# A decoder step on one core: level products merged in the recurrence, prompt attention reordered two heads ahead

## What is computed

```python
# recurrence, per head, one token at a time
sa = einsum('bhij,bhj->bhi', S, -kk_t)
S = S * w_t[:, :, None, :] + sa[..., None] * (kk_t * a_t)[:, :, None, :] + v_t[..., None] * k_t[:, :, None, :]
y = einsum('bhij,bhj->bhi', S, r_t)
# attention of the prompt, per head and branch
s = einsum(q, k) * HEAD_DIM ** -0.5 - slopes * dist          # masked where dist < 0
o = gates[0] * softmax(s_cmp) @ v_cmp + gates[1] * softmax(s_slc) @ v_slc + gates[2] * softmax(s_win) @ v_win
```

## Time and profile before

| | us |
|---|---|
| median of 3 runs | 2620.49 (2618.21 to 2624.07) |
| the profiled execution | 2620.29 |
| its span, first to last instruction | 2618.5 |
| recurrence, from its first matmul to the last chunk's `sa_product` | 214.1 |
| prompt attention | 75.0 |
| from the end of the output projection on | 1058 |

### The profile page before, as it was taken

The page is one execution under the profiler, slowest core; times in us unless marked ns, Lnnn a source line. Parts: engine busy times, 40 slices in busy tenths (PEclk is TensorE's granted clock), DMA queues, the critical chain, the costliest instruction groups (busy, mean ns, idle before and its releaser), DMA issues. The chain is left out here.

```text
span 2618.5 us, 48741 instructions
## 1 busy us (share of the span) xinstructions
PE 2294.2 (88%) x20955; PEld 1646.5 (63%) x20955; DVE 741.7 (28%) x2064; ACT 343.0 (13%) x776; POOL 74.0 (3%) x123
## 2 busy tenths in 40 slices
PE   6899999799999777786776997999999999999996
PEld 4577676677777666755654764566566666556663
DVE  1111211340141245455654124112111112221115
ACT  1001100211210000014322012001010000001001
POOL 0000000000000000001011010000000000000000
PEclk9999999899999967777788998999999999999998
DMA  9987886533444420036468217999999999999990
GB/s 323 346 320 270 332 333 235 163 106 106 129 129 129 120 81 5 5 75 165 159 259 338 78 48 314 424 426 427 426 416 424 426 419 425 426 416 423 424 396 37
DMA packets 205116, 687.62 MB, mean 263 GB/s; under 512 B 38986, under 2 KB 85019, under 8 KB 165371
## 3 DMA queue, kind: packets, MB, share of 16 engines
q1 hardware_dynamic: 195746, 642.59, 62.9%
q0 software_dynamic: 7056, 38.29, 4.3%
q10 hardware_dynamic: 2180, 4.76, 0.5%
HBM read 687.16 MB, written 19.86 MB: 270 GB/s over the span
## 5 line engine op out<-in xcount | busy, mean ns | idle before, releaser
L2761 PE MATMUL bank<-sb_gate_w,sb_x_picked 128*64 128x256 f32 x2048 | 331.2, 389 | 53.6 <-DMA sb_up_w<-in_w_up_dram 53.6
L647 PE MATMUL bank<-sb_hT,sb_sample_kv 128*128 128x296 f32 (+1 forms) x1408 | 355.5, 412 | 12.3 <-PEq L494 12.3
L2761 PE MATMUL bank<-sb_up_w,sb_x_picked 128*64 128x256 f32 x2048 | 330.1, 387 | 0.0
L647 PEld LDWEIGHTS bank<-sb_hT,sb_sample_kv 128*128 128x128 f32 x1408 | 267.9, 191 | 94.7 <-issue 17.5
L2761 PEld LDWEIGHTS bank<-sb_gate_w,sb_x_picked 128*64 128x64 f32 x2048 | 175.4, 140 | 125.8 <-issue 81.7
L2786 PE MATMUL bank<-sb_down_w,sb_hiddenT 128*64 128x512 f32 x1024 | 226.8, 594 | 9.0 <-ACT sb_x_picked L2843 9.0
L469 PE MATMUL bank<-sb_cmp_xT,sb_cmp_w 128*128 128x254 f32 x1024 | 223.3, 379 | 6.6 <-ACT sb_cmp_xT L241 5.8
L469 PEld LDWEIGHTS bank<-sb_cmp_xT,sb_cmp_w 128*128 128x128 f32 x1024 | 193.2, 190 | 38.1 <-ACT sb_cmp_xT L241 7.3
L2761 PEld LDWEIGHTS bank<-sb_up_w,sb_x_picked 128*64 128x64 f32 x2048 | 179.2, 140 | 49.0 <-issue 1.0
L2913 DVE TENSOR_TENSOR sb_hidden<-sb_hidden,bank 128x256 f32<-128x256 f32 x32 | 13.5, 421 | 688.8 <-ACT sb_hidden L2851 688.8
L2786 PEld LDWEIGHTS bank<-sb_down_w,sb_hiddenT 128*64 128x64 f32 x1024 | 84.1, 137 | 129.0 <-issue 115.4
(11 more groups left out here) (569 smaller groups left out, 2340.2 us busy)
## 6 DMA issues: line engine op xcount, KB each, us to landing
sb_gate_w<-in_w_gate_dram SPq DMA_DIRECT2D x64, 2048.0 KB, 16.4
sb_up_w<-in_w_up_dram SPq DMA_DIRECT2D x64, 2048.0 KB, 18.7
sb_down_w<-in_w_down_dram SPq DMA_DIRECT2D x64, 2048.0 KB, 18.2
sb_w_ada<-in_w_ada_dram SPq DMA_DIRECT2D x48, 2048.0 KB, 10.9
sb_sample_kv<-in_w_in_dram SPq DMA_DIRECT2D x22, 2048.0 KB, 8.0
sb_sample_kv<-in_cache_cmp_kv_dram SPq DMA_DIRECT2D x128, 256.0 KB, 7.4
sb_sample_kv<-in_w_out_dram SPq DMA_DIRECT2D x16, 1024.0 KB, 12.2
sb_sample_kv<-in_state_win_kv_dram SPq DMA_DIRECT2D x8, 1024.0 KB, 16.3
```

What stands on the lines that cost most here:

```text
L647: ins = pe.matmul(bank[j % 4][:, 0:wide], ch[:, t, j % 2 * P:(j % 2 + 1) * P], hT[:, t, 0:wide], start=(t == 0), stop=(t == KT - 1))
L2761: ins = pe.matmul(bank[b][64 * half:64 * half + 64, col:col + 256], x[:, t, b * 64:b * 64 + 64], w[i][:, t % CK, half * 256:half * 256 + 256],
```

## The change

Three edits.

1. Recurrence. `pw` gets a third slot, which holds the running sum. Powers and sum are now neighbours, so the products of line 1049 and line 1053 at levels 1 and 2, which have the same stationary operand, become one matmul of 64 columns. All products of a level go to bank 3. Over a chunk, 176 level products become 144. DVE's add writes the sum into the other `pw` tile, and at level 4 into `u.pt`.
2. Prompt attention. The query scale moves into the copies at the end of the input projection (lines 785 and 879), so `scaled` goes. Scores of the selected and window branch become one matmul per tile, the values five matmuls of up to 256 columns instead of eight, DVE's two distance terms one instruction, and the factors of both tiles one pair of instructions. The copy of the compressed part's transpose and `written` move from DVE to ACT. PE issues `scores(0)`, `scores(1)` and then `turned(h)`, `scores(h+2)`, `values(h)`.
3. The samples' queries are multiplied by 1.0 instead of the scale (line 1851).

```diff
@@ phase_in, ACT and DVE @@
-                        act.copy(k.pT[:, j - N_R, 0:NT], bank[j % 4][:, 0:NT]).then_inc(s_copy[0], 1)
+                        act.activation(k.pT[:, j - N_R, 0:NT], bank[j % 4][:, 0:NT], ACT.Copy,
+                                       scale=SCALE if j - N_R < HEADS else 1.0).then_inc(s_copy[0], 1)
...
-                        dve.tensor_copy(k.pT[:, j - N_R, 0:NT], bank[j % 4][:, 0:NT]).then_inc(s_copy[1], 1)
+                        dve.tensor_scalar(k.pT[:, j - N_R, 0:NT], bank[j % 4][:, 0:NT], SCALE if j - N_R < HEADS else 1.0,
+                                          None, ALU.mult).then_inc(s_copy[1], 1)
@@ phase_scan @@
-        pw = [sb(f"pow{i}", [P, 2, Q, CL]) for i in range(2)]
+        pw = [sb(f"pow{i}", [P, 3, Q, CL]) for i in range(2)]
...
-                    if i < 3:
-                        for h in range(HT):
-                            _, _, q, rb = head(h)
-                            ins = pe.matmul(bank[3][rb, P + q * CL:P + (q + 1) * CL], cur[rb, 0, q, :], cur[rb, 1, q, :], start=True, stop=True)
-                    if i > 0:
-                        for h in range(HT):
-                            _, _, q, rb = head(h)
-                            ins = pe.matmul(bank[5][rb, q * CL:(q + 1) * CL], cur[rb, 0, q, :], u.pt[rb, q, :], start=True, stop=True)
+                    lo, hi = (1 if i < 3 else 2), (3 if i > 0 else 2)
+                    for h in range(HT):
+                        _, _, q, rb = head(h)
+                        ins = pe.matmul(levels[rb, lo:hi, q, :], cur[rb, 0, q, :], cur[rb, lo:hi, q, :], start=True, stop=True)
                     ins.then_inc(s_lp, 1)
...
-                        ins = dve.tensor_tensor(full(u.pt), full(u.pt), bank[5][:, 0:P], ALU.add)
+                        sum_ = u.pt[:, :, :] if i == 4 else nxt[:, 2, :, :]
+                        ins = dve.tensor_tensor(fl3(sum_), fl3(cur[:, 2, :, :]), bank[3][:, 2 * P:3 * P], ALU.add)
@@ phase_attend_prompt @@
+                    for t in range(2):
+                        pe.matmul(k.bank[t][:, 0:2 * NK[t]].rearrange("p (a n) -> p a n", a=2), k.pT[:, h, t * P:(t + 1) * P],
+                                  k.pT[:, SLC_T + g:WIN_T + g + 1:WIN_T - SLC_T, 0:NK[t]], start=True, stop=True).then_inc(s_s, 1)
...
                 scores(0)
+                scores(1)
                 for h in range(HEADS):
-                    if h + 1 < HEADS:
-                        scores(h + 1)
                     turned(h)
+                    if h + 2 < HEADS:
+                        scores(h + 2)
                     values(h)
...
+                exps(0, 0)
+                exps(0, 1)
+                normed(0)
+                exps(1, 0)
+                exps(1, 1)
                 for h in range(HEADS):
-                    normed(h)
+                    cmp_copied(h)
                     if h + 1 < HEADS:
-                        exps(h + 1)
+                        normed(h + 1)
+                    if h + 2 < HEADS:
+                        exps(h + 2, 0)
+                    written(h)
+                    if h + 2 < HEADS:
+                        exps(h + 2, 1)
...
                 biased(0)
+                biased(1)
+                factors(0)
                 for h in range(HEADS):
-                    factors(h)
+                    copied(h)
                     if h + 1 < HEADS:
-                        biased(h + 1)
+                        factors(h + 1)
                     if h + 2 < HEADS:
-                        scaled(h + 2)
-                    if h:
-                        written(h - 1)
-                    copied(h)
-                written(HEADS - 1)
+                        biased(h + 2)
```

More of the change, by code:

```diff
@@ new lines, in biased @@
+                        both = lambda w: w.rearrange("p (a n) -> p a n", a=2)
+                        dve.scalar_tensor_tensor(out=v[:, 0:NCP], in0=dcmp[:, t, :], scalar=sl,
+                                                 in1=k.bank[0][:, TP + 16 * t:TP + 16 * t + NCP], op0=ALU.mult, op1=ALU.add)
+                        step(dve.scalar_tensor_tensor(out=both(v[:, 16:16 + 2 * nk]), in0=dist, scalar=sl,
+                                                      in1=both(k.bank[t][:, 0:2 * nk]), op0=ALU.mult, op1=ALU.add))
```

100 lines of the change are left out of this document (45 added, 55 removed).

## The result

| | before | after |
|---|---|---|
| median of five runs, us | 2620.49 (2615.68 to 2625.64) | 2607.70 (2599.71 to 2610.61) |
| the profiled execution | 2620.29 | 2599.71 |
| its span | 2618.5 | 2598.0 |

The ratio is 0.9946, with a 95% interval of 0.9923 to 0.9969, so the changed kernel is faster, by 12.8 us by the medians (8 to 20 us by the interval). The forecast of 2599.3 us lies 8.4 us under the median. That it lies within half a microsecond of the profiled execution is luck: that execution is the fastest of the five, the others took 2607 to 2611 us.

The account below looks back on a forecast made before the run. The prediction took PE's instruction arrival to bound the recurrence, and PE's waits, then SP's DMA stream, the prompt attention: 2620.3 - 11.5 - 9.5 = 2599.3 us, with a range of 2592 to 2612 us.

Parts of the forecast that it names:

- The bound of the recurrence: Recurrence: PE waits for its instructions, arriving in pieces of 256 about every 3.5 us; a chunk can't take under 22.2 us.
- Rival 1: Recurrence: stops stay, only PE's own time counts, about 1 us gained; 2610 us, chance 0.17.
- The size of that term: Recurrence: half a piece of 256 instructions fewer per chunk saves 1.4 us for eight chunks, 0.3 more in the first: 11.5 us.
- What merging costs PE: Recurrence levels: a merged 64-column group takes 0.45 us at the high clock; by PE's own time -1 to +2 us in all.
- The attention's rounds: Prompt attention: the new order removes PE's gap; a round falls from 7.49 to 5.3 us at the high clock, set by ACT.
- The cap: Prompt attention: SP's DMA stream ends the block, so at most its 10.4 us wait for PE is gained; 9.5 us taken.
- Rival 2: Prompt attention: five rounds run at the low clock, so the gain there is 4 us; 2605 us, chance 0.15.
- Rival 4: Recurrence and attention: the clock falls where it is high today, making the kernel slower; 2658 us, chance 0.04.
- Rival 5: Sample attention or experts: the saved time is given back to a wait for DMAs; 2619 us, chance 0.04.

Follow-up runs that it names:

- extra32: The changed kernel with 32 products of one column added in each recurrence chunk, in levels 1 and 2; 2620.48 us, ratio 0.9982 to the kernel before.
- extra64: The changed kernel with 64 products of one column added in each recurrence chunk, in levels 1 and 2; 2635.04 us, ratio 1.0030 to the kernel before.
- scan_only: The kernel before with the new recurrence alone; 2615.32 us, ratio 0.9960 to the kernel before.
- attend_only: The kernel before with everything of the change except the new recurrence; 2619.73 us, ratio 0.9986 to the kernel before.
- after_again: The changed kernel run once more, unedited; 2606.57 us, ratio 0.9940 to the kernel before.
- values_first: The changed kernel with the gates' stores and loads one block earlier, and scores(h+2) issued behind values(h); 2616.39 us, ratio 0.9970 to the kernel before.
- windows_last: The changed kernel with the four window loads moved to the end of SP's stream in the attention; 2600.25 us, ratio 0.9908 to the kernel before.
- gates_in_scan: The changed kernel with the windows' copy moved to the output projection and the gates' DMAs to the recurrence's start; 2584.55 us, ratio 0.9852 to the kernel before.

## Why the prediction was right, and where its sizes were off

**The bound of the recurrence.** Right. Stops stand 128 matmuls apart after as before, and with columns left out of account the number of instructions sets the chunk (extra32, extra64). Rival 1 (the stops stay, only PE's own time counts) falls with scan_only, 10.5 us where it gave about 1.

**The size of that term.** 11.5 us forecast, 10.5 measured (6 to 15). A chunk was to be 21.3 us and is 21.56; stops were to be 2 us a chunk and are 10.7 us in 100 us, 2.3 a chunk. The closeness is in part luck, as two errors cancel. In the profiled pair the seven chunks behind the first give 1.13 us each, 7.9 us, where 1.4 each was forecast. And the way from the first matmul to the second `sa` fell from 56.1 to 51.5 us, 4.6, where the first of the eight chunks and the levels ahead of it were priced at 1.4 + 0.3 = 1.7 us: in that stretch, beside the copy, PE stops with nothing to wait for over 10.0 us before and 9.3 us after. The trace before was also a lucky base: it has the fastest arrival of all fourteen (3547 matmuls in the 100 us from 1000 on, the others 3331 to 3445, so 3.6 us a piece against 3.7 to 3.8), and a slower one makes the half piece worth more.

**What merging costs PE.** The price was right, 0.45 us at the high clock; the sum of -1 to +2 us was never measured by itself. The Trainium skill (TensorEngine Tiling (Array Packing), Instruction Overhead) would have made 64 columns no dearer than 32. The rows disagree there, as said in the prediction, but agree one step below: one column cost as much as 32 (0.43 against 0.44 us for 32 instructions). So these rows show a floor: at the low clock 32 columns cost no more than one, and 64 cost more than 32.

**The attention's rounds.** The mechanism was right, the limiting engine wrong. I had ACT as the bound at 5.3 us a round at the high clock; the round is 4.74 us and PE has no gap, so PE is the bound. ACT's terms were too high: it is busy for 4.20 us a round, copies and all, where I had 4.8 and 0.5 uncovered. It cost the forecast nothing, since the cap decided. The eight rounds were to end 54 us after the block's start and ended after 54.5, by luck: the first transposes came 10.75 us after the start and not 12, the first round took 9.3 us at the low clock, and the others less than 5.3 on the mean.

**The cap.** That SP's stream would end the block was right. The step that failed is the reading of SP's slack as a fixed number. I took 9.5 of 10.4 us; by the profiled pair the block gave 6.0 us, by attend_only the kernel gained 3.7 us (0 to 7). This term carries most of the 8.4 us by which the forecast was too low. SP's 10.4 us of waiting say how much later the heads end than the stream in that one execution. The stream itself took 63.3 us before, 67.5 after, and 64.5 to 67.8 us in attend_only, extra32, extra64, after_again and scan_only, beside DMA engines that are 0.92 busy in after. A term that stands on one execution of a crowded stream should have had a spread of 4 us, and a value below the cap.

**The other rivals.** Rival 2 (low clock rounds) came in part: the first round and the seventh's values ran low, at 9.3 us a round for the first. Behind the cap it cost nothing. Rival 4 (slower through the clock) didn't come; 0.74 and 0.77 are above the 0.70 and 0.75 of before. values_first shows that the order of the same products can decide it in the attention: with the other order the clock falls and 24 us go. Rival 5 (given back to a later DMA wait) isn't in the change, but in windows_last, 5.8 us.

## What to carry to other kernels

Where an engine stops in a run of like instructions with nothing to wait for, count the instructions between the stops. If the count is constant, suspect the stream's own arrival, and test it by adding instructions that do next to nothing. Where it is the bound, as here, fewer instructions are worth more than fewer columns, and a heavy DMA beside the stretch adds a stop. And the slack of a DMA stream beside which an engine is made faster is a number with a spread of its own: once that stream is the bound, look at what stands at its head. Here eight stores of 0.4 KB, moved to a block in which their queue was empty, were worth 16 to 18 us (each with an error of some 8 us), about as much as the whole change, and with the copy moved too the kernel takes 2587 us, 1.45% less than before.

## What the runs showed of the hardware

- Instructions of PE arrive at 3331 to 3547 matmuls with as many loads in 100 us, in fourteen traces and at mean clocks from 0.67 to 0.75, and slower beside a DRAM to DRAM copy of 8.3 MB: 8.1 us for a piece of 256 instead of 3.7, in after. The Trainium skill (Runtime: NRT & Kernel Launch, Instruction fetch mechanics) has the 256 right; that the cost is mostly hidden isn't so in this stretch.
- A matmul of one column in a 32x32 tile costs what one of 32 columns does, 13 ns at the low clock.
- The issue of eight DMAs of 0.4 KB in 4 byte packets held SP for 13.3 to 13.6 us at the head of the attention's block in six traces, for 15.5 us in extra64 and for 23.8 us in after, beside gathers of 8.4 MB on POOL's queue. Without them it held SP for 9.5 to 10.3 us in the block before (five traces) and for 5.4 us at the start of the recurrence (gates_in_scan).
- A gap of 2.6 us in a round of 10.5 us went with a clock of 0.71, no gap with 0.85, one trace each; and after 14.8 us of rest the next block began at 0.61.
